# Expert stage of a two-block model: routing steps between the dot products, dots that signal their own buffer, diagonal matrices from ScalarE

## What is computed

```python
def peer_ffn(h, w_q, sub_keys, expert_u, expert_v):        # 8 heads, 128 + 128 keys, top 16
    q = (ht @ w_q).reshape(n_tok, PEER_HEADS, PEER_QDIM)
    s1 = jnp.einsum('thd,kd->thk', q[..., :half], sub_keys[0])
    s2 = jnp.einsum('thd,kd->thk', q[..., half:], sub_keys[1])
    v1, i1 = lax.top_k(s1, PEER_TOPK)
    v2, i2 = lax.top_k(s2, PEER_TOPK)
    cand = (v1[..., :, None] + v2[..., None, :]).reshape(n_tok, PEER_HEADS, 256)
    cidx = (i1[..., :, None] * PEER_NKEYS + i2[..., None, :]).reshape(n_tok, PEER_HEADS, 256)
    top, pos = lax.top_k(cand, PEER_TOPK)
    eidx = jnp.take_along_axis(cidx, pos, axis=-1)
    gate = jax.nn.softmax(top, axis=-1)
    ...
    u = expert_u[ec]
    act = jax.nn.gelu(jnp.einsum('td,thkd->thk', hc, u), approximate=False)
    return jnp.einsum('thk,thkd->td', gc * act, expert_v[ec])
```

## Time and profile before

| | before |
|---|---|
| median of 3 runs | 3180.43 us (3180.03 to 3184.96) |
| span of the profiled execution | 3392.8 us |
| PE / PEld / DVE / ACT / POOL busy, share of the span | 75% / 55% / 60% / 26% / 34% |
| gathers: instructions on POOL | 2 x 512 |
| expert stage, layer 0 / layer 1: first gather | 286.8 / 1397.6 us |
| TensorE, mean granted clock | 0.873 of 2.4 GHz |

### The profile page before, as it was taken

How to read it: one execution, slowest core, us unless ns; L and a number is a source line. 1 busy time by engine, 2 the same in 40 slices (tenths; PEclk the granted TensorE clock), 3 DMA queues, 4 the chain that set the end, 5 groups by cost and what they waited for, 6 DMA issues and landing times. The chain is left out here.

```text
span 3392.8 us, 37022 instructions
## 1 busy us (share of the span) xinstructions
PE 2551.8 (75%) x12337; PEld 1852.6 (55%) x12337; DVE 2018.8 (60%) x3764; ACT 898.5 (26%) x1120; POOL 1148.3 (34%) x1122
## 2 busy tenths in 40 slices
PE   7878646646647887765755755789898988998898
PEld 6856222222223685722322222379887988997798
DVE  5545766766766553576676676745575553555454
ACT  5333000000000533300000000033464443435443
POOL 2024766666756002466666666600100000000000
PEclk9988878878778888887878877889999998998899
DMA  8517988988889852688988988956525654562364
GB/s 290 163 62 248 346 315 329 340 312 337 333 300 343 280 162 75 224 335 322 352 312 324 356 319 317 346 170 184 161 91 162 185 174 131 171 192 96 103 185 140
DMA packets 448438, 813.43 MB, mean 240 GB/s; under 512 B 27700, under 2 KB 298662, under 8 KB 448326
## 3 DMA queue, kind: packets, MB, share of 16 engines
q0 software_dynamic: 148240, 538.89, 42.1%
q1 hardware_dynamic: 300086, 273.10, 25.9%
HBM read 810.85 MB, written 1.05 MB: 239 GB/s over the span
## 5 line engine op out<-in xcount | busy, mean ns | idle before, releaser
L1391 PE MATMUL ps<-weight_ring,arena 128*128 128x512 f32 x2048 | 965.7, 633 | 606.0 <-PEq L1388 575.8
L1391 PEld LDWEIGHTS ps<-weight_ring,arena 128*128 128x128 f32 x2048 | 411.6, 204 | 1159.9 <-issue 1158.9
L644 POOL DMA_INDIRECT arena<-in_peer_u,expert x512 | 549.3, 1073 | 587.6 <-POOLq L643 430.9
L1937 DVE CUSTOM_DVE_ANT_0 h_ext<-arena,h_ext 128x1024 f32<-128x1024 f32 x512 | 627.4, 1225 | 117.6 <-DVE dots L1937 53.7
L1184 PE MATMUL ps<-hT_hi,ring_lo 128*128 128x256 f32 (+1 forms) x2112 | 606.0, 287 | 0.0
L650 POOL DMA_INDIRECT weight_ring<-in_peer_v,expert x512 | 519.0, 1014 | 156.2 <-issue 144.9
L1668 DVE TENSOR_TENSOR ring_lo<-weight_ring,w_hi 128x3072 fp32r<-128x3072 f32 (+1 forms) x104 | 332.1, 3194 | 253.4 <-DVEq L1667 253.3
L1182 PE MATMUL ps<-hT_hi,w_hi 128*128 128x256 f32 x1536 | 441.2, 287 | 15.1 <-PEq L1408 13.1
L1183 PE MATMUL ps<-hT_lo,w_hi 128*128 128x256 f32 x1536 | 440.3, 287 | 0.0
L1184 PEld LDWEIGHTS ps<-hT_hi,ring_lo 128*128 128x128 f32 (+1 forms) x2112 | 411.3, 195 | 0.0
L1182 PEld LDWEIGHTS ps<-hT_hi,w_hi 128*128 128x128 f32 x1536 | 300.7, 196 | 20.2 <-issue 17.0
(11 more groups left out here) (320 smaller groups left out, 3674.2 us busy)
## 6 DMA issues: line engine op xcount, KB each, us to landing
weight_ring<-in_w_ada SPq DMA_DIRECT2D x32, 1536.0 KB, 7.7
weight_ring<-in_ffn_w_gate SPq DMA_DIRECT2D x88, 512.0 KB, 4.0
weight_ring<-in_ffn_w_up SPq DMA_DIRECT2D x88, 512.0 KB, 5.3
weight_ring<-in_ffn_w_down SPq DMA_DIRECT2D x88, 512.0 KB, 5.8
weight_ring<-in_peer_wq SPq DMA_DIRECT2D x16, 1024.0 KB, 5.5
weight_ring<-in_w_in SPq DMA_DIRECT2D x12, 1024.0 KB, 6.0
weight_ring<-in_rg_w_in SPq DMA_DIRECT2D x12, 896.0 KB, 5.1
weight_ring<-in_w_out SPq DMA_DIRECT2D x8, 1024.0 KB, 4.9
```

Of the source, the lines that this page charges most:

```text
L644: g.indirect_dma_start(u_ring[:, k % U_SLOTS, :], None, A["peer_u"], bass.IndirectOffsetOnAxis(expert[:, p, k:k + 1], 0)).then_inc(u_in[k ...
L1391: ins = mm(ps[:, 2 * t + c, :], diag[:, k, :], v_ring[:, k, c * N:(c + 1) * N], start=False, stop=False, skip_group_check=True)
L1937: v.tensor_tensor_reduce(out=junk, in0=u_ring[:, j, :], in1=h[:, t, :], scale=1.0, scalar=0.0, op0=ALU.mult, op1=ALU.add, accum_out=dots[: ...
```

## The change

VectorE's `route` is cut into sixteen small functions, which each issue one or two steps and return the count of `dve_steps` that the next one has to wait for. `unit` now writes them between the dots. In the first half of unit n stand the last steps of unit n+1 (`pairs_at` to `rows_known`), in the second half the first steps of unit n+2 (`keys_high` to `close_top`). So unit n+1's `expert_ready` is set at the end of unit n's first half, and its maxima one unit earlier. Unit 0 and the maxima of unit 1 are routed ahead of the stage.

A dot writes its product over the slot of `u_ring` that it reads, signals `u_free` itself and isn't waited for; `dots_ready` is set once the engine has drained. The two one-hot passes over 256 columns become one over 512. ScalarE copies the scores (`next_scores`) and builds the diagonals, as sixteen activations with act times gate as the scale; VectorE keeps the small product `mixing` (`weigh`), for the first half after the third dot of the second half, for the second half after the third dot of the next unit. The wait on `diag_free` moves to ScalarE.

```diff
-                def unit(t, n, p, follow):
-                    for g in range(2):
-                        for j in range(GRP):
-                            dve.wait_ge(u_in[j], (l * (2 * UNITS) + (n * 2 + (g + 1))) * 16)
-                            v.tensor_tensor_reduce(out=junk, in0=u_ring[:, j, :], in1=h[:, t, :], ...
-                                                   ... accum_out=dots[:, g, j:j + 1]).then_inc(dve_steps, 1)
-                            dve.wait_ge(dve_steps, steps.next())
-                            dve.sem_inc(u_free, 1)
-                        dve.sem_inc(dots_ready, 1)
...
-                        for j in range(GRP):
-                            k = g * GRP + j
-                            v.tensor_scalar(diag[:, k, :], ident[:], acts[:, g, j:j + 1], gate[:, k:k + 1], ...
...
-                            if follow:
-                                route(n + 1, 1 - p)
+                def dot(t, n, g, j):
+                    dve.wait_ge(u_in[j], (l * (2 * UNITS) + (n * 2 + (g + 1))) * 16)
+                    v.tensor_tensor_reduce(out=u_ring[:, j, :], in0=u_ring[:, j, :], in1=h[:, t, :], ...
+                                           ... accum_out=dots[:, g, j:j + 1]).then_inc(u_free, 1)
+                def weigh(g):
+                    dve.wait_ge(acts_ready, 1)
+                    dve.sem_inc(acts_ready, -1)
+                    v.tensor_tensor(mixing[:, g, :], acts[:, g, :], gate[:, g * GRP:(g + 1) * GRP], ALU.mult)...
+                def unit(t, n, p, before=True, follow=2):
+                    dot(t, n, 0, 0)
+                    if follow >= 1:
+                        at = pairs_at(1 - p)
+                    dot(t, n, 0, 1)
+                    if follow >= 1:
+                        at = places(at)
+                    dot(t, n, 0, 2)
+                    if before:
+                        weigh(1)
...
+                    dot(t, n, 1, 0)
+                    if follow == 2:
+                        dve.wait_ge(half_ready, 1)
+                        dve.sem_inc(half_ready, -1)
+                        high = [keys_high(s) for s in range(2)]
+                    dot(t, n, 1, 1)
+                    if follow == 2:
+                        left = [keys_left(s, high[s]) for s in range(2)]
+                    dot(t, n, 1, 2)
+                    dve.wait_ge(dve_steps, gated)
+                    weigh(0)
...
+                def diagonals(half):
+                    act.wait_ge(mixing_ready, 1)
+                    act.sem_inc(mixing_ready, -1)
+                    act.wait_ge(diag_free, 1)
+                    act.sem_inc(diag_free, -1)
+                    for j in range(GRP):
+                        a.activation(diag[:, half * GRP + j, :], ident[:], ACT.Copy, scale=mixing[:, half, j:j + 1])...
```

More of the change, by code:

```diff
@@ L1905, in best_pairs @@
-                    v.scalar_tensor_tensor(expert_f[:], chosen[:, 0, :], float(KEYS), chosen[:, 1, :], ALU.mult, ALU.add).then_inc(dve_steps, 1)
-                    dve.wait_ge(dve_steps, steps.next())
-                    v.tensor_scalar(expert[:, p, :], expert_f[:], expert_base[:], None, ALU.add).then_inc(expert_ready, 1)
[L1909 to L1913, removed]
-                    best_pairs(p)
+                    return steps.next()
@@ new lines, in choices, with numbers @@
+                def choices(after):
+                    dve.wait_ge(dve_steps, after)
+                    v.tensor_reduce(chosen[:].rearrange("p s k -> p (s k)"), onehot.rearrange("p s k j -> p (s k) j"), AX_X, ALU.add).then_inc(dve_steps, 1)
+                    return steps.next()
+                def numbers(after):
+                    dve.wait_ge(dve_steps, after)
+                    v.scalar_tensor_tensor(expert_f[:], chosen[:, 0, :], float(KEYS), chosen[:, 1, :], ALU.mult, ALU.add).then_inc(dve_steps, 1)
+                    return steps.next()
@@ L1919, in _ @@
                     low(u, in_hi, KC * BLK)
[L1920 to L1927 removed]
+                scores_here(0)
@@ L1967, in _ @@
-                with dve.Fori(0, EXPERT_HEADS // 2) as i:
-                    for p in range(2):
-                        unit(0, i * 2 + p, p, True)
+                scores_here(1)
+                high = [keys_high(s) for s in range(2)]
+                left = [keys_left(s, high[s]) for s in range(2)]
+                more = [keys_low(s, left[s]) for s in range(2)]
+                at = pair_sums(more[1])
+                for s in range(2):
+                    keys_high_at(s, high[s])
+                at = pairs_left(1, pairs_high(1, at))
@@ new lines, in _ @@
+                for s in range(2):
+                    keys_low_at(s, more[s])
+                close_top(1, pairs_low(1, at))
+                dve.sem_inc(dve_steps, -steps.reset())
+                def dot(t, n, g, j):
+                    dve.wait_ge(u_in[j], (l * (2 * UNITS) + (n * 2 + (g + 1))) * 16)
+                    v.tensor_tensor_reduce(out=u_ring[:, j, :], in0=u_ring[:, j, :], in1=h[:, t, :], scale=1.0, scalar=0.0,
+                                           op0=ALU.mult, op1=ALU.add, accum_out=dots[:, g, j:j + 1]).then_inc(u_free, 1)
@@ L1970, in _ @@
+                unit(0, 0, 0, before=False)
+                with dve.Fori(0, EXPERT_HEADS // 2 - 1) as i:
+                    for q in range(2):
+                        unit(0, i * 2 + (1 + q), 1 - q)
+                unit(0, EXPERT_HEADS - 1, 1)
                 dve.sem_inc(params_free, 1)
-                with dve.Fori(0, EXPERT_HEADS // 2 - 1) as i:
-                    for p in range(2):
-                        unit(1, i * 2 + (EXPERT_HEADS + p), p, True)
+                unit(1, EXPERT_HEADS, 0)
@@ L1974, in _ @@
+                with dve.Fori(0, EXPERT_HEADS // 2 - 2) as i:
+                    for q in range(2):
+                        unit(1, i * 2 + (EXPERT_HEADS + 1 + q), 1 - q)
                 dve.wait_ge(y_ready, 1)
```

252 lines of the change are left out of this document (172 added, 80 removed).

## The result

The changed kernel takes 3255.9 us (median of four, 3242.6 to 3260.2), the kernel before 3182.7 beside it (3180.0 to 3194.8): ratio 1.0227, 95% interval 1.0205 to 1.0250. It is slower by 73 us. The forecast had slower, by 140.

A forecast was written before the change was run, and what follows sets the result against it. Timed runs were taken as bound by GpSimd's gather issues, 43.4 us a unit rising to 48.7. Per layer: units 1 to 13 pay 69, unit 14 1, unit 15 gives 2, start and end 2; both +140, 3320 (3100 to 3400).

The forecast's parts named there:

- the pauses belong to the profiled execution: VectorE's routing: 9.7 us of pauses a unit were taken to occur only under the profiler, leaving its loop 41.7.
- a unit of 43.4: GpSimd's issue path before the change: 39.7 for 32 gathers, 2.9 for 16 dots, about 0.4 for first dots.
- Rival 1: VectorE's pauses exist without the profiler too; a unit goes from 51.4 to 48.7, 3105 us, faster; chance 0.20.
- The span forecast, 3317: Profiled span of the changed kernel: 76 us less, as units go from 51.4 to 48.7 and the pauses go.
- The hold of the issues: A gather's issue, 0.13 us in, waits for the end of a running VectorE operation with two SBUF inputs.
- rival 2: Dots do not hold gather issues; VectorE's 41.7 was the base and DMA's 40.9 bounds, 3158 us; chance 0.06.
- the price of the steps between the dots and of the first dot of each half: Issue path per unit: 7.6 us for gaps made by routing steps, 1.4 for the two halves' first dots.
- 1.25 + w: Spacing of issues beside dots with a gap w below 1.24 us: one issue per dot, each paying w extra.
- Plain dots: Dots without steps between, only in unit 15: the 0.19 us gap between them goes, giving 2 us.
- Start and end: Expert stage of a layer: start 0 to 3 us, end 0 to 5 us, together 2 in the sum.
- Diagonals on ScalarE: VectorE loses 4.3 us a unit and the Gelu wait; sixteen diagonals cost ScalarE 3 to 12 us, hidden.
- Rivals 3 and 4: 3: dots 1.42 apart, steps not overlapping, 3420, chance 0.10; 4: two issues per dot, 3195 to 3230, chance 0.06.

The follow-up runs named there:

- b_again: The kernel before, unchanged, profiled once more: time 3179.2 us, span 3177.5.
- p_scalar: The kernel before with only the diagonals built on ScalarE, from acts x gate multiplied on VectorE: 3189.5 against 3177.4 us, ratio 1.0040.
- p_short: The kernel before with eleven routing steps left out, gathering other rows but as many: 3164.6 against 3177.4 us, ratio 0.9958.
- a_psum: The changed kernel with h copied to PSUM by ScalarE and read there by the dots from unit 1 on: 3130.6 us, 0.9837 of the kernel before.
- a_rows: The changed kernel with routing steps, gate and multiplications behind each half's eight dots instead of between them: 3120.8 us, 0.9828 of the kernel before.
- a_tail: The changed kernel with `weigh(0)` moved ahead of the second half's dots: 3265.8 us, 0.9563 of the kernel before, which took 3413.5 in that comparison.
- a_rows_psum: The changed kernel with all steps behind the dots and h read from PSUM: 3281.2 us, 0.9618 of the kernel before at 3413.5.

## Why the prediction came out as it did

**The bound and the base.** The step "the pauses belong to the profiled execution" was wrong: b_again is profiled and has none, and seven executions of the last comparison lie at 3413. What was drawn from it, a unit of 43.4 bound by issues in the timed runs, held: 43.6 in b_again, and p_scalar and p_short show that VectorE's work is worth nothing there. That is luck in part: the timed runs happened to lie at the level without pauses, for a reason that the prediction did not have. Rival 1 is true of the other level: there a kernel one line away from the changed one is 4.4% faster. Had the changed kernel been timed there, the sign would probably have been the other. The span forecast, 3317, took the pauses for a part of profiling and was 67 us too high (3250.2). Nor are there 11 us "around the span": in each profiled execution whose time is on record the time stands 1.7 to 1.8 above the span, and the two profiles of this kernel differ by 215, not 224. The range's text counts rival 1 (3050 to 3150) once as mostly inside 3100 to 3400 and once as half outside; half is right.

**The hold of the issues.** Right in its mechanism: a_psum takes the second SBUF input away and the 1.43 become 0.93 (rival 2 falls); a_rows takes the gaps away and 73 us of loss become 57 of gain.

**The mis-sized term** is the price of the steps between the dots and of the first dot of each half, 7.6 + 1.4 = 9.0 a unit. In units 1 to 13 of layer 0 the issues are 46.0 us apart per unit, 6.3 above the free 39.7. This 6.3 comes out of the dots' timeline: a half has seven gaps between dots and not eight, the dots are 1.614 us apart on average in the first half and 1.691 in the second, and 7 x (1.614 - 1.24) + 7 x (1.691 - 1.24) = 5.8. The prediction's 1.25 + w gave 1.69 and 1.76. Its 1.25 stood in no row; a dot gives way to the next operation after 1.13, and the range had that as its lower end (1.17) while the sum took the upper. The rule that a step starts 0.08 before its forerunner's end was read off two rows that have 0.11 and 0.02; the changed kernel has 0.08 to 0.09 ahead of the dots shown above, so the rule held. And the first dot of a half costs an issue 0.24 on average over layer 0 (0 to 0.98), 0.5 a unit, not 1.4; in more than half of the cases it is 0.1 or less, as if the dot, which waits for a landing, came in step with the issues.

**Plain dots** (unit 15, "gives 2 us"): right in sign, 2.5 measured. That "nothing but unit 15 has plain dots" was right for the changed kernel and hid its lesson: plain dots 1.28 apart cost next to nothing, and a_rows has them everywhere. Unit 14, forecast at +1, gives 1.3 and 0.8: only its first half has steps between the dots.

**Start and end, 2 a layer.** The start cost 3.1 and 0.7 (a first issue 0.7 later, a unit 0 longer by 2.4 and 0.7); 0 to 3 had been given. The end cost 7.7 and 7.1, the range given being 0 to 5: TensorE needs 14 to 16 us for each half, and in the last unit it begins the first one only when the third dot of the second half has released it:

```profile
1015.40 15.69 PE L1427 MATMUL ps<-weight_ring,arena 128*128 128x512 f32 x32 [5.00 <-ACT arena L955]
1031.35 13.97 PE L1427 MATMUL ps<-weight_ring,arena 128*128 128x512 f32 x32 [0.26 <-PEq L1424]
```

The second follows the first without a rest, though VectorE released it at 1021.29. In a_rows, where the release stands ahead of the second half's dots, the end is 14.2. (a_tail, meant to show this alone, fell on the other level: 21.2 and 19.8, with pauses in it.)

**Diagonals on ScalarE.** Eight take 2.45 us, in the range given, hidden; the Gelu wait went with them, to no gain at this level.

**Rivals 3 and 4** did not happen: no chain of VectorE's, and one gap in 182 with two issues.

The whole sum, both layers, forecast against the difference between the profiles of the changed kernel and of b_again:

| | forecast | measured |
|---|---|---|
| units 1 to 13 | +138 | +60.6 (2.4 and 2.3 a unit, not 5.3) |
| unit 14 | +2 | -2.1 |
| unit 15 | -4 | -5.1 |
| start, unit 0 | start and end together: +4 | +3.8 |
| last issue to the sum with x | | +14.8 |
| all else | 0 | +0.7 |
| sum | +140 | +72.7 |

So the sign and the mechanism were right at this level, the main term was put at more than twice its size, and the end of the stage at far too little. The second error makes up for a part of the first, by luck.

## What to carry to other kernels

Where GpSimd issues gathers beside VectorE operations with two SBUF inputs, look at how the issues fall between them: evenly spaced operations just over an issue apart (1.28 against 1.24) cost next to nothing, each gap added between them is paid in full (seen up to 1.80 apart), and operations packed closer than an issue (1.15) cost three tenths of the issues' rate. Where the issues bound the time, as they do here at 3180, short steps therefore belong behind such a row, not inside it, even if the row's engine idles nearly half its time; reading one operand from PSUM lifts the whole matter. And a profile whose span stands 7% above the timed median is a profile of another condition: profile again before anything is built on it.

## What the runs showed of the hardware that was not expected

- Dots 1.15 apart let two issues through in three dots (1.98 and 0.94 us), dots 1.28 apart one each (0.97).
- The same program ran at 3180 and at 3413 us, each level stable within 0.5% to either side over a whole comparison; at the higher one steps that waited only for a finished step of their own engine started up to 4.8 us late (L1943 in a_rows_psum) while the DMA engines were full.
- A row of dots that only waits for landings takes their pace, 1.28 us (0.524 MB at 410 GB/s), which is just over an issue's 1.24, so that the two hardly collide.
